# Attention with queries on partitions for the values and their sums, and scores in steps of four key tiles

## The reference, cut to what matters

```python
# sequence 2048, width 2048, 8 attention heads, 128 (nope) + 64 (rope) channels per query and key
q_all = (rms_norm(a_cq, cq_norm[l]) @ w_uq[l]).reshape(B, S, A_HEADS, A_DQK)
q_rope = apply_rope(q_rope, ...); k_rope = apply_rope(a_kr, cos, sin)      # k_rope is shared by the heads
kv = (rms_norm(a_ckv, ckv_norm[l]) @ w_ukv[l]).reshape(B, S, A_HEADS, A_NOPE + A_DV)
ha = causal_block_attention(qa, ka, v_a) * jax.nn.silu(a_z)   # causal softmax(q k / sqrt(192)) v, then the gate
hm = mlstm_chunkwise(mq, mk, mv, ig, lf) ...                  # branch A
hc = memory_attention(...) * jax.nn.silu(c_z)                 # branch C
merged = g_m * (hm @ w_br_m[l]) + g_a * (ha @ w_br_a[l]) + g_c * (hc @ w_br_c[l])
x = x + merged @ w_out[l]
return rms_norm(x, final_norm)
```

## Time and profile before

| | us |
|---|---|
| runs without a profile | 2771.6, 2772.2, 2772.23 (median 2772.2) |
| the profiled execution | 2748.97 |
| its span (slowest core, core 1) | 2747.7 |
| spans of the eight cores | 2732.5 to 2747.7 |
| PE busy in the span | 2693.6 |

### The profile page before, as it was taken

The page is one execution under the profiler, slowest core; times in us unless marked ns, Lnnn a source line. Parts: engine busy times, 40 slices in busy tenths (PEclk is TensorE's granted clock), DMA queues, the critical chain, the costliest instruction groups (busy, mean ns, idle before and its releaser), DMA issues.

```text
span 2747.7 us, 41837 instructions; the slowest of 8 cores (2732.5 to 2747.7 us)
## 1 busy us (share of the span) xinstructions
PE 2693.6 (98%) x14037; PEld 1300.4 (47%) x14037; DVE 1059.3 (39%) x1788; ACT 892.9 (32%) x1741; POOL 617.0 (22%) x924
## 2 busy tenths in 40 slices
PE   7999899999999999999999999999999999999998
PEld 3544344564446644454555444444444444444444
DVE  6645377548576556244434311111111111111433
ACT  5532356436565454254544211111111111110212
POOL 0003100100210121277760122222222222221000
PEclk9999999999999999999999999999999999999999
DMA  9657724532544324556645744445475544447562
GB/s 252 130 131 159 193 62 108 117 98 55 105 104 108 78 41 86 96 141 155 166 107 147 170 77 76 78 74 79 77 165 92 95 75 77 76 78 131 193 206 87
DMA packets 142211, 312.38 MB, mean 114 GB/s; under 512 B 14833, under 2 KB 73009, under 8 KB 134961
## 3 DMA queue, kind: packets, MB, share of 16 engines
q0 software_dynamic: 42048, 134.27, 30.6%
q1 hardware_dynamic: 95634, 162.32, 18.9%
q10 hardware_dynamic: 4320, 13.11, 1.5%
HBM read 371.22 MB, written 72.68 MB: 162 GB/s over the span
## 4 chain that ended last, share of the span: by engine, by line
PE 92%; DMA 5%; ACT 1%; DVE 1%; issue 1%; POOL 1%; SPq 0%; ACTq 0%; POOLq 0%; DVEq 0%
PE bk L290 91%; DMA xt<-x 1%; DMA xo<-x 1%; DMA QRT<-ob 1%; DMA cz<-CZ 0%; DMA HMT<-hm 0%; PE bk L514 0%; SPq L135 0%; DMA QNT<-ob 0%; DMA mb<-BH 0%; PE bk L535 0%; PE bk L1188 0%; PE bk L1234 0%; DVE ro L303 0%; PE bk L1338 0%
## 5 line engine op out<-in xcount | busy, mean ns | idle before, releaser
L290 PE MATMUL bk<-hT,wg 128*128 128x512 bf16 x3072 | 682.3, 380 | 0.0
L290 PE MATMUL bk<-w,hT 128*128 128x512 bf16 (+1 forms) x3072 | 598.3, 345 | 7.5 <-DMA w<-wA 2.9
L290 PE MATMUL bk<-hT,w 128*128 128x512 bf16 x2112 | 489.6, 380 | 0.0
L290 PEld LDWEIGHTS bk<-hT,wg 128*128 128x128 bf16 x3072 | 300.5, 98 | 361.5 <-issue 1.6
L290 PEld LDWEIGHTS bk<-w,hT 128*128 128x128 bf16 x3072 | 296.3, 98 | 251.8 <-issue 16.2
L294 ACT ACTIVATE sh<-bk 128x512 f32<-128x512 f32 x184 | 109.8, 597 | 850.1 <-PE bk L290 850.1
L290 PE MATMUL bk<-hb,wb 128*128 128x512 bf16 x1536 | 346.7, 379 | 0.0
L290 PEld LDWEIGHTS bk<-hT,w 128*128 128x128 bf16 x2112 | 204.9, 98 | 228.8 <-issue 4.7
L310 DVE SCALAR_TENSOR_TENSOR tm<-sh,bk 128x512 f32<-128x512 f32 x124 | 85.3, 688 | 559.2 <-PE bk L290 559.2
L290 PEld LDWEIGHTS bk<-hb,wb 128*128 128x128 bf16 x1536 | 150.1, 98 | 181.1
L303 DVE TENSOR_TENSOR den<-den,Pa 128x512 f32<-128x512 f32 (+3 forms) x288 | 186.4, 647 | 103.4 <-ACT Pa L294 75.1
(11 more groups left out here) (180 smaller groups left out, 2433.1 us busy)
## 6 DMA issues: line engine op xcount, KB each, us to landing
wg<-wGB POOLq DMA_DIRECT2D x96, 512.0 KB, 5.3
w<-wA POOLq DMA_DIRECT2D x48, 516.0 KB, 9.2
wb<-wGB POOLq DMA_DIRECT2D x96, 256.0 KB, 4.1
xt<-x SPq DMA_DIRECT2D x16, 1024.0 KB, 13.3
xo<-x SPq DMA_DIRECT2D x16, 1024.0 KB, 6.8
out<-xo SPq DMA_DIRECT2D x15, 1024.0 KB, 7.4
wo<-wOUT POOLq DMA_DIRECT2D x4, 2048.0 KB, 17.5
w<-wA POOLq DMA_DIRECT2D x16, 500.0 KB, 12.2
```

The costliest lines, as they stand in the source:

```text
L290: fw.op("pe", lambda e: e.matmul(bk[o] if not isinstance(o, bass.AP) else o, lhsT=lhsT, rhs=rhs, start=start, stop=stop), reads=reads, wri ...
```

## The change

Attention: `emit_S` takes four key tiles at a time, with all nope matmuls first, then all rope matmuls, then the masks. Steps run across blocks and heads in one list (`groups`), and the scores of the next step are issued before the values of this one. For the values `Pa` is now stationary, 128 queries at a time, and `vx` moves with 129 columns, the last a column of twos that yields the sum (`VA` is stored 130 wide for that). The result has queries on partitions: DVE takes a reciprocal of the sum column and applies it and the gate in one operation for each 128 queries (`fin_half`); four PE transposes turn the block back (`finish`). `den`, `hia`, `loa`, Ln and Exp are gone. The gate `az` is projected with tokens on partitions (`gate_block`) and stored in pieces of 128 elements. Two fixed banks (`PO`) hold the values of a block, two query tiles each.

Around it: query stores of `uq` go out by halves, and attention's first loads wait for the mark `UQ3` instead of `UQ0`; the mLSTM starts its preparation at `V1` and its chunks at the second tile of `oz3`; its `mg` loads are issued half a chunk later, and `HMT` is stored from ACT's queue; `ho` has four buffers; the first four `wb` loads are spread; `gfin` and the last output weights are loaded later; the last tile is scaled by DVE in three parts and ACT in one.

```diff
@@ p1_gen, block uq
-                    for ci in (2, 0, 1):
+                    for ci in ((2, 0, 1) if pr or tb else (0, 1, 2)):
...
-                for ci in range(2):
-                    hh = 2 * pr + ci
-                    fw.dma("sp", QNT_d[hh * 128:(hh + 1) * 128, :], o3[ci][:], reads=[o3[ci].r], accs=[dr("QNT", hh)])
-                fw.dma("sp", QRT_d[pr * 128:(pr + 1) * 128, :], o3[2][:], reads=[o3[2].r], accs=[dr("QRT", pr)])
-                if pr == 0:
-                    marks.add("UQ0")
+                    if tb % 2:
+                        c = slice(tb * 512 - 512, tb * 512 + 512)
+                        for ci in range(2):
+                            hh = 2 * pr + ci
+                            fw.dma("sp", QNT_d[hh * 128:(hh + 1) * 128, c], o3[ci][:, c], reads=[o3[ci].rs[tb // 2]], accs=[dr("QNT", hh)])
...
+                        if pr == 3 and tb == 1:
+                            marks.add("UQ3")
@@ gate_block
+            for t_ in range(NT):
...
+                yield from tm_unit(w, 512, lambda kc: htile(kc, t_), [rh[t_]],
+                                   lambda bk, r_bk: silu2_evac(bk, r_bk, AZ_d[4 * blk:4 * blk + 4, :, t_, :].rearrange("h p c -> p h c"), dr("AZ", blk, t_ // 4), 4))
@@ mla_gen
+            def fin_half(hb_, az, hq):
+                po, r_po = PO[hb_]
+                rd = rds.next()
+                pv = po[:, 0:260].rearrange("p (b c) -> p b c", b=2)
+                fw.op("dve", lambda e: e.reciprocal(out=rd[:], in_=pv[:, :, 128:129].rearrange("p b c -> p (b c)")), reads=[r_po], writes=[rd.r])
+                for j in range(2):
+                    b = 2 * hb_ + j
+                    stt(hq[:, b, :], pv[:, j, 0:128], rd[:, j:j + 1], az[:, b, :], ALU.mult, ALU.mult, [r_po, rd.r, az.r], [hq.r] if b == 0 else [], [hq.r] if b else [])
...
+            groups = [(h, qb, kq) for h in range(8) for qb in range(4) for kq in range(qb + 1)]
...
+                for k, n, qc, kc_, (bs, r_bs) in its:
+                    mm(bs, r_bs, (slice(None), slice(0, n)), kn[:, kc_], qn[:, qc], True, False, [kn.r, qn.r])
+                for k, n, qc, kc_, (bs, r_bs) in its:
+                    hf = slice(64 * (k % 2), 64 * (k % 2) + 64)
+                    mm(bs, r_bs, (slice(None), slice(0, n)), kr[hf, kc_], qr[hf, qc], False, kq < qb, [kr.r, qr.r])
...
+                if gi + 1 < len(groups):
+                    nxt = emit_S(*groups[gi + 1])
+                    yield 6 * MM
+                vx = vxs[h % 2]
+                for k, p, n in cur_:
+                    b0 = 4 - n // 128
+                    for b in range(b0, 4):
+                        po, r_po = PO[b // 2]
+                        c = (b % 2) * 130
+                        mm(po, r_po, (slice(None), slice(c, c + 129)), p[:, (b - b0) * 128:(b - b0 + 1) * 128], vx[:, k, 0:129], ...
+                    if k >= 4 * qb and k % 2:
+                        fin_half(k % 4 // 2, az, hq)
+                    tick()
+                    yield MM * n / 512
+                if kq == qb:
+                    finish(h, qb, hq)
@@ mlstm_gen
-                loads_g(c + 2)
...
-                    fw.dma("sp", HMT_d[cp // 4, :, cp % 4, :], hm2[0][:].rearrange("p a b -> p (a b)"), reads=[hm2[0].r], accs=[dr("HMT", cp // 4)])
+                    fw.dma("act", HMT_d[cp // 4, :, cp % 4, :], hm2[0][:].rearrange("p a b -> p (a b)"), reads=[hm2[0].r], accs=[dr("HMT", cp // 4)])
...
+                if c > 0:
+                    loads_g(c + 1)
@@ dense_all and the end
-        sides = [(mla_gen, "MLA0", 0.38), (mlstm_gen, "ML", 0.34), (c_gen, "CZ0", 0.7)]
+        sides = [(mla_gen, "MLA0", 0.38), (mlstm_gen, "V1", 0.34), (c_gen, "CZ0", 0.7)]
...
-                    if n4 % 2:
+                    if n4:
```

More of the change, by code:

```diff
@@ L687, in p1_gen, with part, half @@
             cqnT, ckvnT = P["cqnT"], P["ckvnT"]
-            ob = Ring(tiles("ob", 6, [128, S], BF16))
-            def part(o, c, bk, r_bk, first):
-                evac_copy(o[:, c], bk[:, 0:512], [r_bk], [o.r] if first else [], [] if first else [o.r])
+            ob = Ring(tiles("ob", 6, [128, 2080], BF16, n=2))
+            def part(o, tb, bk, r_bk):
+                evac_copy(o[:, tb * 512:(tb + 1) * 512], bk[:, 0:512], [r_bk], *half(o, tb))
+            def half(o, tb):
+                return ([], [o.rs[tb // 2]]) if tb % 2 else ([o.rs[tb // 2]], [])
             def rotate(o, tb, bk, r_bk):
@@ L1025, in f4, with finish @@
+            def finish(h, qb, hq):
+                def f1():
+                    bt, r_bt = SBk.next()
+                    btb = b16(bt, 8)
+                    for b in range(4):
+                        fw.op("pe", lambda e: e.transpose(out=btb[:, b, :], in_=hq[:, b, :], identity=identb[:]), reads=[hq.r, RC], writes=[r_bt])
                     o = has.next()
-                    tt("dve", o[:], u[:], rb[:], ALU.mult, [u.r, rb.r], [o.r])
+                    copy("dve", o[:].rearrange("p (b c) -> p b c", b=4), btb[:, 0:4, :], [r_bt], [o.r])
@@ new lines, in finish, with emit_S @@
+                later(3, f1)
+            groups = [(h, qb, kq) for h in range(8) for qb in range(4) for kq in range(qb + 1)]
+            def emit_S(h, qb, kq):
+                i = h % 2
+                qn, qr, kn = qns[i], qrs[i], kns[i]
+                its = []
+                for k in range(4 * kq, 4 * kq + 4):
+                    n = (4 * qb + 4 - max(k, 4 * qb)) * 128
+                    its.append((k, n, slice(4 * qb * 128 + 512 - n, 4 * qb * 128 + 512), slice(k * 128, (k + 1) * 128), SBk.next()))
+                for k, n, qc, kc_, (bs, r_bs) in its:
[4 more added lines that the diff above has]
+                if kq == qb:
+                    for k, n, qc, kc_, (bs, r_bs) in its:
+                        mm(bs, r_bs, (slice(None), slice(0, 128)), identb[:], mneg[:], False, True, [RC, mneg.r])
+                res = []
+                for k, n, qc, kc_, (bs, r_bs) in its:
+                    p = Ps.next()
+                    act(p[:, 0:n], bs[:, 0:n], AF.Exp, [r_bs], [p.r], scale=SC)
+                    res.append((k, p, n))
+                return res
@@ L1586, in d_gen @@
                 xload(t)
+                if t == 3:
+                    fw.dma("sp", gfin[:], gf_d, writes=[gfin.r])
+            for r in cur[2].rs:
+                fw.wait_res("pool", r)
+            wo_load(3, wo3)
             for n4 in range(4):
```

176 lines of the change are left out of this document (57 added, 119 removed).

## The result

The change makes the kernel slower: 2787.8 us against 2772.2, a ratio of 1.0055 (95% interval 1.0037 to 1.0073). The medians are over all runs, the ratio is over those in which no half of the chip ran at a lower clock than the other. The prediction was 2742, a ratio of .9891. Later runs on another chip, where the kernel before takes 2750, give 1.0077 (1.0064 to 1.0091).

The account below looks back on a forecast made before the run. PE, busy 2693.6 of 2747.7 us, was taken as the bound. PE's work -20.0, stalls that go -14.5 and new waits +4 summed to -30.5: 2718.5 profiled, 2742 us without a profile, range 2726 to 2763.

Parts of the forecast that it names:

- PE's work: Attention on PE: value products +2.6, sum matmuls gone -13.8, transposes +7.2, rope steps -16; together -20.0 us.
- the first rival: Attention's scores: third and fourth rope matmuls wait for weights, .10 a step, +8 us, time 2750; chance 0.20.
- the term by itself: Attention's scores: 80 steps of four key tiles instead of 160 of two, each saving .20 on the rope pair, -16 us.
- The stalls in `uq`: Block `uq`: later attention loads and buffers freed by halves remove PE's wait behind `ob`, -6.0 us (bounds 0, -6.8).
- the smaller pieces of `AZ`: Gate stores of 256-byte pieces: hidden, cost nothing; a doubled landing of 26 us would pass the ring's 20 by up to 6.
- that for `Pa`: Start of attention: first value products no longer directly follow their exp, -1.5 us of the 2.2 behind `Pa`.
- The new waits: Attention's block changes: PE waits for DVE to empty the value banks, +4 us (0 to 35).
- a new row of waits behind the reciprocal of over 10 us: Attention, PE's waits in the new trace: a sign that would make the prediction wrong.
- The rival on the score banks: Attention: scores wait for ACT's four exps to empty all four banks; at .8 us a step, time 2805; chance 0.06.
- `hm`: mLSTM: storing from ACT's queue shortens PE's wait behind ACT's copy into `hm`, -5.0 of 6.2 us.
- -10.5 of standing still: Whole kernel: stalls that go, -14.5 us, and waits that may come anew, +4.
- The 23.2 us: Whole kernel: median without a profile, 2772.2, over the profiled execution, 2748.97; added to the predicted 2718.5.

Follow-up runs that it names:

- e5: e3 with each block's gate tile `az` loaded one block earlier; ratio .9888 to the kernel before.
- e0: The kernel before the change, run again without edit on a later chip; ratio 1, span 2747.2 us.
- e4: The changed kernel, run again without edit on a later chip; ratio 1.0077 to the kernel before, span 2772.9 us.
- e7: e5 with scores in steps of two key tiles instead of four; ratio .9963 to the kernel before.
- e1: The changed kernel with `VA` stored in 512-byte pieces, the column of twos set once in each `vx` tile; ratio .9982 to the kernel before.
- e3: The changed kernel with 512-byte `VA` pieces as in e1 and the transposed block copied by ACT instead of DVE; ratio .9936 to the kernel before.
- e10: The changed kernel with 512-byte `VA` pieces without gaps in `ob`, at 520-byte distances in DRAM; `VA` landing 32.7 us, ratio not given.

## Why the prediction was wrong

**PE's work: right.** Predicted -20.0 us; e5 has 23.3 less than e0, so the two agree within a few us. The 3.3 between them were not taken apart; the granted clock from 200 to 300 us, .98 in e0 and 1.00 in e5, may be a part. In e4, whose clock is lower, only 13.9 show. Value products stand .23/4 = .0575 apart and transposes .22/4 = .055 (timeline above, 872.19 and 874.43), where .0565 and .056 were taken. Four rope matmuls take .54, two take .32 (timelines of e5 and e7): the second pair follows .22 behind the first, as assumed, and the first rival (a wait for weights, .10 a step) is out. e7 measures the term by itself: 16.2 for 16.

**The stalls in `uq`: the step that failed first.** The prediction said: "With the loads at the end of the block, by when that store has long landed, and with buffers freed by halves, I take -6.0; bounds 0 [...] and -6.8." e4 waits 24.6 us there (13.5 + 7.7 + 3.4), and the bounds did not hold it. The query stores do land sooner; but `ob` is shared with the `VA` stores just ahead, and the prediction costed neither their 130 columns nor anything else of `uv`. It weighed the smaller pieces of `AZ`, whose stores land in 2.2 us (median in e5), not the 26 of its estimate, and for which PE waits nowhere in e5, and passed over the odd ones, which cost 26 us. With even pieces (e1) the waits behind `ob` and `ro` go, but the loads held to `UQ3` queue ahead of the last stores and cost 6.5 behind `Pa`. So even without the odd pieces the term and that for `Pa`, -7.5 together, are not reached: PE waits 6.5 us from 200 to 320 us in e5, and before the change 8.9 in the first trace (6.8 behind `ob`, 1.5 and .6 behind `Pa` and `ro`) but 4.5 in e0 (3.0 and 1.5). That is a gain of 2.4 or a loss of 2.0: the 6.8 of the earlier trace rows was one execution's, and more than half of it was not there in the next.

**The new waits: mis-sized, +4 for 23.4.** "DVE must be about 4 us late for PE to feel it" fits the two value banks (in e3 DVE's scaling is 8.22 us late, and PE waits 4.27), and is wrong as the only place. The prediction had named a new row of waits behind the reciprocal of over 10 us as a sign against it, and it came: 11.7. The rival on the score banks named ACT's exps as what empties them and gave it .06; that four scores share their ring with the transposes, and that DVE frees that bank, was in the code (`SBk.next()` in `finish`) and in no sum. DVE's busy share, 475 of 740 us, was read as relief; what counts is what stands ahead of one copy in its list, here 5 us, from the transposes at 874.43 to 879.61. The third new wait, the late `az`, has the same form on SP; DVE waits 7.9 us for `az` in e4 and 23.4 in e3, where the bank no longer holds PE up; that the bank hid it before is argued.

**`hm`: right in place, -5.0 at the upper end in size.** Its 6.2 us are gone, but `kw` now takes 3.3 for 1.3, and `Cf` 2.2 in the first trace. Behind `hm`, `kw`, `Cf` and ACT's `hmt` together PE waits 8.0 and 9.4 us before the change (first trace and e0), 5.5 and 5.2 in the two traces of the change, and 4.2 in e5, so 2.5 to 5.2 are gained. Which of the edits in the mLSTM does it was not tested one by one.

**The sum.** For the change as written it forecast -20.0 of PE's work and -10.5 of standing still; e4 against e0 shows -13.9 and +39.6. -30.5 is what e5 gains (2749.97 to 2719.28 is -30.7), but that is luck: e5 has three repairs that the prediction did not know, and another division, -23.3 from PE's work and -5.4 from standing still. As written, the change waits longer than e5 by 24.6 us in `uv` and `uq`, by 20.5 behind `rda` and `ha` (23.4 for 2.9) and by 1.6 behind `Pa` (8.1 for 6.5), 46.7 together; PE stands still 45.0 longer by the table. The 23.2 us by which the prediction raised its time, from the first trace to the runs, belong to the first chip: in e0 the execution of the trace takes 2748.6, and the median of the runs on the later chips is 2750.0 to 2752.4. Their cause stays open.

## What to carry to other kernels

When a store's row grows by a few bytes, look at where each piece then begins, not at the bytes (in DRAM by e10; for SBUF alone no run shows it): keep the pieces as they were and set the extra column once at the place where it is read. When a step takes all the banks of a ring, list every other user of that ring and the engine that empties it, and look at what stands ahead of that in its in-order list. A small load or copy that frees a shared resource should not stand behind large ones: moving one of .41 us to another engine gave 19 us, and one load a block earlier 13.

## What the runs showed of the hardware

Stores whose pieces begin at multiples of 520 bytes in DRAM landed in 28.9 to 32.7 us (median), where those of 512 bytes took 4.3 and 4.6: some seven times as late. A part of that is waiting behind earlier stores of the same kind. The DMA engines' time for what was moved tells more. From 214 to 222 us, when no other store or load of SP is issued, SP's queue shows (packets, MB, packet time as a share of 16 engines' span), before and after:

```profile
q1 hardware_dynamic: 2080, 1.05, 45.9%
```
```profile
q1 hardware_dynamic: 1403, 0.72, 123.9%
```

The packets overlap, so a share can pass 100%. By the byte it is 3.9 times the packet time. The Trainium skill, DMA: Bandwidth & Descriptors, How a descriptor splits into AXI transactions, says that the first transaction of a piece which does not start at a multiple of 256 bytes begins at the multiple below, and that the bytes before the start are fetched for nothing. By its table that is 25 beats for 18 with 576 bytes; as an estimate from that page, under half more, where the trace shows 3.9 times. So the direction agrees, and the size does not follow from it.

A long wait can cost more than its length, since the granted clock falls while PE stands still. In e5, behind the wait of 6.50 us:

```profile
309.76 1.01 PE L290 MATMUL bk<-qn,kn 128*128 128x512 bf16 x2 [6.50 <-ACT Pa L294]
310.70 1.04 PE L290 MATMUL bk<-qr,kr 64*128 64x512 bf16 x4
311.67 5.22 PE L290 MATMUL bk<-w,hT 128*128 128x512 bf16 x16
316.73 0.68 PE L290 MATMUL bk<-vx,Pa 128*128 128x129 bf16 x9
```

The sixteen dense matmuls take 316.73 - 311.67 = 5.06 us instead of 16 x .216 = 3.46, their cost at the full clock of 2.4 GHz, and the scores ahead of them 1.91 instead of .53 for two nope matmuls and .54 for four rope ones: 2.4 us on top of 6.5. The granted clock is 1.00 from 300 to 303 us, .78 from 306 to 309.7, still in the wait, .50 right behind it, which is the lower level of 1.2 GHz, and 1.00 again once PE has worked for some us:

```profile
309.70:311.70 2.00, 1.94 (x7) 0.37 (x8) 0.69 (x1) 0.87 (x3) 0.00 (x0) 0.50 0.99 228
316.70:320.00 3.30, 3.30 (x24) 1.84 (x23) 0.84 (x4) 0.60 (x1) 0.00 (x0) 1.00 0.17 40
```

Not every wait does it: in the first trace of the changed kernel PE waits 3.27 us for `kw`, and the clock from 1229.5 to 1233 us is 1.00.

In e4 the stretch from 200 to 300 us has a granted clock of .88, in e5 1.00, and over the whole span e4 is 9.4 us busier than e5 with the same products. So about 45 us of standing still and 9 of busy time make up the 54 between the spans of these two; that the 9 are all clock is argued from the stretches, not measured by itself.
